# Scaled copies of the token shift in SBUF, the merged tiles split inside their own stage, and splits moved ahead of stage ends

## What is computed

```python
h = x @ w_in[l]                      # cut into rwkv, latent attention, convolution, memory and merge columns
p_prev = jnp.pad(p, ((0, 0), (1, 0), (0, 0)))[:, :-1]
p = p + mu * (p_prev - p)            # the token shift, at the start of the rwkv branch
...
branches = jnp.stack([y_rwkv, y_mla, y_conv, y_mem], axis=2)
proj = jnp.einsum('bsnc,ncd->bsnd', branches, w_o_branch[l])
gates = jax.nn.sigmoid(merge.reshape(B, S, N_BRANCH, D) + b_gate[l])
merged = jnp.sum(gates * proj, axis=2)
out = merged @ w_out[l]
x = _layer_norm(DEEPNORM_ALPHA * x + out, ln_g[l], ln_b[l])
```

## Time and profile before

| what | value |
|---|---|
| median of 3 runs (lowest to highest) | 3420.7 us (3420.3 to 3421.48) |
| the profiled execution's own time | 3420.07 us |
| its span, from the first to the last instruction | 3418.3 us |
| PE busy | 3225.6 us, 94% |
| DVE, ACT, POOL busy | 44%, 35%, 44% |
| mean granted TensorE clock | 0.982 of full speed |
| from HBM | 278.75 MB, 82 GB/s over the span |

### The profile page before, as it was taken

One profiled execution on the slowest core, in us unless ns is written; L12 is line 12 of the kernel. 1 busy time (PEld: TensorE's weight loads), 2 busy tenths in 40 slices (PEclk: granted clock), 3 DMA queues, 4 the chain that ended last, 5 costly groups with the idle time before them and its releaser, 6 DMA issues. The chain is left out here.

```text
span 3418.3 us, 51762 instructions
## 1 busy us (share of the span) xinstructions
PE 3225.6 (94%) x21116; PEld 2532.1 (74%) x21116; DVE 1500.7 (44%) x2378; ACT 1188.0 (35%) x1940; POOL 1488.2 (44%) x820
## 2 busy tenths in 40 slices
PE   8899998999898999989998988999999989899999
PEld 6784786788577747867886756888888876678787
DVE  6633374898666333848896236210000022520000
ACT  6234433422362334343223435322112233532221
POOL 4431553454344225534552258333334433845454
PEclk9999999999999999999999999999999999999999
DMA  3011121555210111325552210212111111023232
GB/s 127 9 34 55 56 99 62 209 191 200 76 62 3 39 55 51 106 86 189 200 185 85 87 32 2 68 62 62 62 62 62 62 60 56 1 87 99 93 99 93
DMA packets 77611, 284.18 MB, mean 83 GB/s; under 512 B 8736, under 2 KB 8736, under 8 KB 76864
## 3 DMA queue, kind: packets, MB, share of 16 engines
q1 hardware_dynamic: 77376, 280.88, 24.4%
HBM read 278.75 MB, written 2.10 MB: 82 GB/s over the span
## 5 line engine op out<-in xcount | busy, mean ns | idle before, releaser
L131 POOL TENSOR_TENSOR lows<-ring,highs 128x1024 fp32r<-128x1024 f32 x376 | 939.1, 2498 | 1607.3 <-ACT highs L123 1590.4
L155 PE MATMUL ps<-x_high,highs 128*128 128x512 f32 x1936 | 771.6, 399 | 36.2 <-ACT highs L123 17.4
L158 PE MATMUL ps<-x_low,highs 128*128 128x512 f32 x1936 | 758.7, 392 | 0.0
L123 ACT ACTIVATE highs<-ring 128x1024 fp32r<-128x1024 f32 x376 | 396.9, 1056 | 749.9 <-PE ps L155 388.4
L155 PEld LDWEIGHTS ps<-x_high,highs 128*128 128x128 f32 x1936 | 366.2, 189 | 127.1 <-issue 30.7
L158 PEld LDWEIGHTS ps<-x_low,highs 128*128 128x128 f32 x1936 | 365.9, 189 | 78.3 <-issue 3.5
L2744 DVE TENSOR_TENSOR hidden_scratch<-ps,hidden_scratch 128x512 f32<-128x512 f32 x44 | 30.4, 692 | 546.0 <-PE ps L2063 541.5
L677 PE MATMUL ps<-x_high,lows 128*128 128x512 f32 x1040 | 256.8, 389 | 0.0
L677 PEld LDWEIGHTS ps<-x_high,lows 128*128 128x128 f32 x1040 | 195.3, 188 | 40.5
L2620 DVE SCALAR_TENSOR_TENSOR BR<-ps,mod,BR 128x512 f32<-128x512 f32 x72 | 47.4, 662 | 368.8 <-PE ps L167 368.8
L167 PE MATMUL ps<-hidden_parts,lows 128*128 128x512 f32 (+1 forms) x528 | 188.8, 358 | 0.0
(11 more groups left out here) (435 smaller groups left out, 5917.5 us busy)
## 6 DMA issues: line engine op xcount, KB each, us to landing
ring<-in_w SPq DMA_DIRECT2D x414, 512.0 KB, 3.5
merging<-in_ada SPq DMA_DIRECT2D x48, 512.0 KB, 3.5
BR<-in_ada SPq DMA_DIRECT2D x48, 512.0 KB, 3.5
X<-in_xT SPq DMA_DIRECT2D x4, 512.0 KB, 6.7
X<-in_memT SPq DMA_DIRECT2D x2, 1024.0 KB, 5.3
merging<-in_cond SPq DMA_DIRECT2D x4, 512.0 KB, 4.7
out<-BR SPq DMA_DIRECT2D x8, 256.0 KB, 4.4
cst<-in_cst SPq DMA_DIRECT2D x1, 1408.0 KB, 7.7
```

What stands on the lines that cost most here:

```text
L123: nc.scalar.activation(self.high(n), self.chunk(n), ACT.Copy).then_inc(self.hi_made, 1)
L131: nc.gpsimd.tensor_tensor(self.low(n), self.chunk(n), self.high(n).bitcast(F32), ALU.subtract).then_inc(self.lo_made, 1)
L155: mm = nc.tensor.matmul(ps, high, xhigh, start=start, stop=False)
L158: nc.tensor.matmul(ps, high, xlow, start=False, stop=False)
```

## The change

It does six things, in both layers where nothing else is said.

- Token shift: ACT's scaled copy goes to `kept` in SBUF, two tiles in turns, in place of its bank. Its wait for its own eviction goes. PE's waits for a bank, and the one ahead of the gram matmuls, are for the copy (`kept`) and no longer for the mix.
- The first pair of tiles: PE takes k = 0, 1 of tile 0 first and waits for tile 1's high weights only after it.
- The splits of the chunk that the next stage opens with move ahead of the last evictions of ACT (latent projections, memory values).
- Merge: high and low parts of merged tiles 0 to 6 are made in the merge stage, and PE makes the high-weight matmuls of output tiles 0 and 1 for k = 0 to 6 there. To make room, `CB`, `GATE`, `WEIGHTED`, `MG` and two of the row buffers lie in the branch tiles' memory `BR`; there are three row buffers for four, three gates for four and two merged tiles for eight. SP orders its transfers anew.
- Output: x is put together (high + low) before the product arrives, so that one DVE step follows a product where there were two. The last tile isn't added to `RUN`; PE adds the sum of `RUN` and the last tile into one bank.
- Context (layer 1): its normalisation starts one output tile earlier, and its transfer waits for nothing.

```diff
-            nc.tensor.matmul(PS[:, 6, :], C("ones", P), self.run, start=True, stop=True).then_inc(S("sum"), 1)
+            nc.tensor.matmul(PS[:, 6, :], C("ones", P), self.rows[:, 7, :], start=False, stop=True, skip_group_check=True).then_inc(S("sum"), 1)
...
+        kept = X[:, 43 * T + 2 * 513:45 * T + 2 * 513].rearrange("p (c t) -> p c t", c=2)
...
+            for j, k in [(j, k) for ks in ((0, 1), *((k,) for k in range(2, DK))) for j in range(2) for k in ks]:
+                if k == 0:
+                    stream.wait_high(pe, n0 + j)
                 pe.wait_ge(before.S("x_low"), k + 1)
-                for j in range(2):
-                    with_high(nc, PS[:, j, :], tile_of(stream.high(n0 + j), k), XH[:, k, :], XL[:, k, :], k == 0)
+                with_high(nc, PS[:, j, :], tile_of(stream.high(n0 + j), k), XH[:, k, :], XL[:, k, :], k == 0)
...
-                    pe.wait_ge(R("mixed"), i - 3)
+                    pe.wait_ge(R("kept"), i - 3)
...
-                act.wait_ge(R("evicted"), i + 1)
-                a.activation(PS[:, i % 4, :], PS[:, i % 4, :], ACT.Copy, scale=less_mu[:, RW_ORDER[i]:RW_ORDER[i] + 1]).then_inc(R("kept"), 1)
+                a.activation(kept[:, i % 2, :], PS[:, i % 4, :], ACT.Copy, scale=less_mu[:, RW_ORDER[i]:RW_ORDER[i] + 1]).then_inc(R("kept"), 1)
...
-                                       in1=PS[:, i % 4, :], op0=ALU.mult, op1=ALU.add).then_inc(R("mixed"), 1)
+                                       in1=kept[:, i % 2, :], op0=ALU.mult, op1=ALU.add).then_inc(R("mixed"), 1)
...
-                pe.wait_ge(R("mixed"), RW_TILES)
+                pe.wait_ge(R("kept"), RW_TILES)
...
+                    if q == 1:
+                        stream.hi(nc, act, n0 + 11 + 1)
                     act.wait_ge(S("v"), q + 1)
                     a.activation(VV[:, q, :], PS[:, q % 2, :], ACT.Copy).then_inc(S("v_out"), 1)
-                stream.hi(nc, act, n0 + 11 + 1)
...
+                stream.hi(nc, act, nm + 8 + 1)
                 for q in range(2):
                     act.wait_ge(S("value"), q + 1)
                     a.activation(VX[:, q, :], PS[:, 4 + q, :], ACT.Copy).then_inc(S("value_out"), 1)
-                stream.hi(nc, act, nm + 8 + 1)
...
+        kept = ExitStack()
+        MH, ML = (kept.enter_context(nc.sbuf_tensor(f"merged_{part}{layer}", [P, DK, T], F32R, side="right"))[:, :, :] for part in ("high", "low"))
+
+        def flat(a, n):
+            return BR[:, a:a + n, :].rearrange("p a t -> p (a t)")
+
+        CB, GATE, WEIGHTED = flat(0, 4).rearrange("p (c k) -> p c k", c=2), BR[:, 4:7, :], BR[:, 7, :]
+        MG, PROD = BR[:, 8:10, :], flat(10, 2)
+        AD = mods[:, layer, :].rearrange("p (m c) -> p m c", c=2)
+        ROWS = (Y[:, :], flat(12, 2), flat(14, 2))
...
+                stream.send(sp, n0 + RING)
+                clear(sp, other)
+                sp.dma_start(rows_of(0), A["ada"][layer, 0, :, :]).then_inc(S("rows0"), 16)
+                sp.wait_ge(S("branch_low"), 4)
                 for c in range(2):
                     sp.dma_start(CB[:, c, :], A["cond"][c].partition_broadcast(P)).then_inc(S("cond"), 16)
...
+                for t in range(1, 48):
                     stream.send(sp, n0 + RING + 45 * t // 48)
-                    if t >= 4:
-                        sp.wait_ge(S("ada"), 2 * (t - 3))
-                    elif t >= 2:
-                        sp.wait_ge(S("branch_low"), 4 + 4 * t)
-                    sp.dma_start(rows_of(t), A["ada"][layer, t, :, :]).then_inc(S(f"rows{t % 4}"), 16)
+                    if t < 3:
+                        sp.wait_ge(S("branch_low"), 12 + 2 * t)
+                    else:
+                        sp.wait_ge(S("ada"), 2 * (t - 2))
+                    sp.dma_start(rows_of(t), A["ada"][layer, t, :, :]).then_inc(S(f"rows{t % 3}"), 16)
...
+                for t in range(2):
+                    pe.wait_ge(S("gate"), 29 + t)
+                    stream.wait_high(pe, n0 + 48 + t)
+                    for k in range(7):
+                        pe.wait_ge(S("merged_low"), k + 1)
+                        with_high(nc, PS[:, t, :], tile_of(stream.high(n0 + 48 + t), k), MH[:, k, :], ML[:, k, :], k == 0, used if t == 0 and k == 0 else None)
...
+                    if i >= 3:
+                        act.wait_ge(S("weighted"), i - 2)
+                    else:
+                        act.wait_ge(S("branch_low"), 5 + i)
+                    nc.scalar.activation(GATE[:, i % 3, :], PS[:, i % 4, :], ACT.Sigmoid, bias=par_col("b_gate", 8 * (i % 4) + i // 4)).then_inc(S("gate"), 1)
                     stream.hi(nc, act, min(gate_chunk(i) + (4 if i % 2 else 3), n0 + 48 + 1))
+                    if i >= 4 and i % 4 == 0:
+                        act.wait_ge(S("merged"), 3 * i // 4)
+                        nc.scalar.activation(MH[:, i // 4 - 1, :], MG[:, (i // 4 - 1) % 2, :], ACT.Copy).then_inc(S("merged_high"), 1)
                     if i == 0:
                         for b in range(8, 16):
                             branch_high(b)
                         act.wait_ge(S("cond"), 32)
                         nc.scalar.activation(CB, CB, ACT.Silu).then_inc(S("silu_c"), 1)
+                stream.hi(nc, act, n0 + 48 + 2)
...
+                    if i == 0:
+                        dve.wait_ge(S("branch_low"), 16)
+                    if n:
+                        dve.wait_ge(S("merged"), 3 * m + n - 1)
+                    v.tensor_tensor(WEIGHTED if n else MG[:, m % 2, :], PS[:, 4 + i % 4, :], GATE[:, i % 3, :], ALU.mult).then_inc(S("weighted"), 1)
                     if n:
                         dve.wait_ge(S("weighted"), i + 1)
-                        if n > 1:
-                            dve.wait_ge(S("merged"), 3 * m + n - 1)
-                        v.tensor_tensor(MG[:, m, :], MG[:, m, :], WEIGHTED[:, n, :], ALU.add).then_inc(S("merged"), 1)
+                        v.tensor_tensor(MG[:, m % 2, :], MG[:, m % 2, :], WEIGHTED, ALU.add).then_inc(S("merged"), 1)
...
+                    if i >= 5 and n == 1:
+                        dve.wait_ge(S("merged_high"), m)
+                        v.tensor_tensor(ML[:, m - 1, :], MG[:, (m - 1) % 2, :], MH[:, m - 1, :].bitcast(F32), ALU.subtract).then_inc(S("merged_low"), 1)
+                    for t in range(min(48, 48 * i // 29), min(48, 48 * (i + 1) // 29)):
+                        dve.wait_ge(S(f"rows{t % 3}"), 16 * (t // 3 + 1))
                         for c in range(2):
                             if 2 * t + c:
                                 dve.wait_ge(S("ada"), 2 * t + c)
                             v.tensor_tensor_reduce(PROD, rows_of(t), CB[:, c, :], 1.0, 0.0, ALU.mult, ALU.add, AD[:, t, c:c + 1]).then_inc(S("ada"), 1)
...
+                if t < 2:
+                    pe.wait_ge(S("merged_low"), 1)
+                    with_high(nc, PS[:, t, :], tile_of(stream.high(n0 + t), 7), MH[:, 7, :], ML[:, 7, :], False, stream.used if t else None)
+                    stream.wait_split(pe, n0 + t)
                     for k in range(DK):
-                        pe.wait_ge(S("merged_low"), k + 1)
-                        with_high(nc, PS[:, 0, :], tile_of(stream.high(n0), k), MH[:, k, :], ML[:, k, :], k == 0, stream.used if k == 0 else None)
-                    stream.wait_split(pe, n0)
-                    for k in range(DK):
-                        mm = nc.tensor.matmul(PS[:, 0, :], tile_of(stream.low(n0), k), MH[:, k, :], start=False, stop=(k == DK - 1))
+                        mm = nc.tensor.matmul(PS[:, t, :], tile_of(stream.low(n0 + t), k), MH[:, k, :], start=False, stop=(k == DK - 1))
...
+            pe.wait_ge(S("run"), 6)
+            nc.tensor.matmul(PS[:, 6, :], ones_matrix, RUN, start=True, stop=False, skip_group_check=True).then_inc(S("run_summed"), 1)
...
+            v.tensor_tensor(ML[:, 7, :], BR[:, 9, :], MH[:, 7, :].bitcast(F32), ALU.subtract).then_inc(S("merged_low"), 1)
             for t in range(8):
+                v.tensor_tensor(RR[:, t, :], XH[:, t, :].bitcast(F32), XL[:, t, :].bitcast(F32), ALU.add).then_inc(S("x_whole"), 1)
                 dve.wait_ge(S("product"), t + 1)
-                v.scalar_tensor_tensor(out=RR[:, t, :], in0=XH[:, t, :].bitcast(F32), scalar=DEEP_ALPHA, in1=PS[:, t % 4, :], op0=ALU.mult, op1=ALU.add).then_inc(S("residual_high"), 1)
-                dve.wait_ge(S("residual_high"), t + 1)
-                v.scalar_tensor_tensor(out=RR[:, t, :], in0=XL[:, t, :].bitcast(F32), scalar=DEEP_ALPHA, in1=RR[:, t, :], op0=ALU.mult, op1=ALU.add).then_inc(S("residual"), 1)
-                if t:
+                dve.wait_ge(S("x_whole"), t + 1)
+                v.scalar_tensor_tensor(out=RR[:, t, :], in0=RR[:, t, :], scalar=DEEP_ALPHA, in1=PS[:, t % 4, :], op0=ALU.mult, op1=ALU.add).then_inc(S("residual"), 1)
...
-            if t == 5:
+            if t == 4:
                 dve.wait_ge(S("c_in"), 16)
                 dve.wait_ge(S("c_rstd"), 1)
                 for k in range(4):
                     normed(k)
```

(2 more changed lines are left out.)

67 lines of the change are left out of this document (18 added, 49 removed).

## The result

| | before | changed |
|---|---|---|
| median (lowest to highest), 7 runs each | 3420.94 us (3420.3 to 3430.33) | 3402.9 us (3398.34 to 3411.73) |
| ratio | | 0.9946, interval 0.9935 to 0.9956 |
| profiled execution, span | 3420.07, 3418.3 us | 3402.9, 3401.1 us |

What follows compares the result with a forecast made beforehand. PE bounds the kernel, busy 3225.6 of 3418.3 us, so only its waits, matmuls and clock count. The terms sum to -33.6 us, mostly from the borders: 3420.7 - 33.6 = 3387.1 us, with 8 in 10 for 3374 to 3401.

Steps and rivals of the forecast that it cites:

- the one on the merge stage: Merge stage: DVE's seven added subtractions and ACT's seven copies a layer cost PE nothing, with three us of slack.
- The start of the merge stage: Gate product 2's chunk, sent behind row 1, lands later: a loss of 1.3 us a layer (0 to 2.5), +2.6 in all.
- Opening: Layer 0's start: four matmuls run ahead and the clock may rise sooner, -1.4 us (0.9 to 2.1 gained).
- Token shift: Token shift: ACT's copy into SBUF gives -0.2 us, mixes of tiles 9 and 10 under POOL +1.2, both layers together.
- Rival 4: Token shift: mixes wait out POOL in every tile and DVE passes it on; 3423 us or more, chance 0.03.
- The moved splits: Latent stage and memory values: earlier splits shorten PE's border waits, -6.9 and -5.8 us over two layers.
- the clock, 0.7 a pair of borders: Latent and memory borders: shorter PE waits may keep the clock up, 0 to 2 us a pair, -1.4 in all.
- Merge to output: Border from merge to output stage: 28 matmuls follow at once, one wait remains; -6.5 us a layer, -13.0 in all.
- End of the output stages: Output stages' ends: fewer DVE steps on the path, shorter waits, some clock; -2.5 us in layer 0, -6.2 in layer 1.
- (2): Merge stage gets tight: ACT's wait for the merged tile or DVE's eighth step delays high splits; 3401 us, chance 0.13.
- (1): At the borders the clock stays up and POOL isn't in the way; 3369 us, around 3374 for most, chance 0.13.
- (3): Latent and memory borders: moved splits do nothing, since another engine ends the stage as late; 3401 us, chance 0.04.

Runs made afterwards that it cites:

- merged_copy_later: The changed kernel with ACT's high copy of a merged tile moved behind the next gate and its split: 3405.82 us, ratio 0.9957.
- moved_splits_alone: The kernel before with only the two moved splits (latent stage, memory values): 3409.38 us, ratio 0.9968.
- also_at_the_start: The changed kernel with every merge-stage weight chunk sent one row earlier, gate product 2's ahead of row 1's wait too: 3388.91 us, ratio 0.9911.

## Why the prediction was wrong, step by step

**The step that failed** is the one on the merge stage, "so I cost it at nothing". It priced the work that was added to ACT and DVE, and found it harmless, rightly: the copy moved away gave next to nothing back, and with SP's chunk a row earlier PE had no wait in the steady part although all the added work was there. What it did not price is the place of the weight chunks in SP's queue. It did look at SP's order, but only at the start, with "Behind SP's wait stand also row 2 and the next chunk, which have 5 us to spare". With three row buffers for four every row, and every chunk behind it, waits until one row more is summed, and this was not followed past the start. Measured were +12.5 and +10.4 us for the stages in place of +1.3 each: 7.0 and 6.2 in the steady part, which was forecast at nothing, and 5.5 and 4.2 at the start. The chunk a row earlier gave the steady part back whole. The start came back with the two further edits, by stage length 9.2 us with its chunk (3.6 of them because PE reached gate product 2 earlier, the rest with the clock) and 3.2 with the split ahead of the silu. With these the time is 3380.8; the forecast for a merge stage at nothing was 3387.1 - 2.6 = 3384.5.

**The start of the merge stage** was forecast as a loss of 1.3, a term that was mis-sized. In layer 0, PE reached gate product 2 2.7 us later by its marks (21.50 us from the start for 18.81). It ran the first part behind it, to the next L1658, in 17.55 in place of 14.74 us, at the lower level: 0.79 and then 0.63 us a record where there were 0.50 and then 0.39. That makes 5.5 in all, where my upper end was 2.5. The stage also opens partly at the lower level (0.64 at 586.55 for 0.47 at 597.31), 1.6 us longer to the first pair of branch products. But this cost nothing, since PE waits for the chunk behind it anyway: in the run merged_copy_later the stage opened at the full level, PE's wait was 4.72 us in place of 3.12, and it reached gate product 2 after 21.47 us.

**Opening**: -1.4 forecast, -1.8 measured. PE starts at 7.72.

**Token shift**: the size was right, +1.0 forecast, no difference measured, and the reason half right. The mixes with two inputs in SBUF do wait out POOL. DVE's groups, changed kernel:

```profile
L845 DVE SCALAR_TENSOR_TENSOR X<-X,par 128x512 f32<-128x512 f32 x26 | 25.0, 963 | 42.8 <-ACT X L797 42.8
```

and before:

```profile
L846 DVE SCALAR_TENSOR_TENSOR X<-X,par,ps 128x512 f32<-128x512 f32 x26 | 19.3, 743 | 50.5 <-ACT ps L798 50.5
```

Five of the 26 did so. In layer 0 tile 1 took 1.44 us, tile 5 2.89 and tile 9 1.78 (at 88.89, beside the first of POOL's four operations of 1.74 us from 88.37 on); in layer 1 tile 1 took 1.43 and tile 9 1.78. Of tiles 9 and 10, where I had put them at +0.73 each, tile 9 came 1.05 us longer and tile 10 met nothing (0.74 at 98.42, POOL's split having ended at 97.95). The times show no cost of them, and DVE has 43 us of idle time ahead of the mixes. By the rule of the Trainium skill (SBUF — State Buffer, "Who interferes with whom"), that a VectorE instruction with two SBUF inputs and a GpSimd one that reads SBUF get in each other's way, such mixes had to come; the trace agrees. Rival 4 failed because five of 26 met POOL and not all, and those had DVE's idle time ahead of them. That the size came out is in part luck. PE's gram wait fell from 4.33 to 2.76, but a new one of 1.61 for L883 stands 4 us ahead of it. ACT's scaled copy was not cheaper in SBUF:

```profile
L797 ACT ACTIVATE X<-ps,less_mu 128x512 f32<-128x512 f32 x26 | 17.7, 681 | 0.0
```

It takes 0.68 for 0.66 in its bank. The prediction's "about 0.60" took a copy without a scale for one with it. The page on ScalarE that I had set aside, by which ScalarE is faster into PSUM than into SBUF, was right in its sign (the Trainium skill, ScalarE: Activation LUTs, "Step-by-step: what each stage is for"). The 0.1 us a tile came from the wait that went: the second copy starts 0.50 behind the first, not 0.63.

**The moved splits**: the waits as forecast (0.94 and 1.23 for "about 1 and 1.5"), 3.5 and 3.1 us. The term mis-sized is the clock, 0.7 a pair of borders: behind the latent border the attention ran 3.0 us faster, since the lower level that it had before is not there (L330's row is 1.55 us for 2.90). These 3.0 us (12.2 for 15.2 from the border to 335.33) are the same in layer 0 of all eleven kernels with the moved splits. The lower level at the start of the merge stage is not their price: the run moved_splits_alone opens it at the full level in both layers, as do the runs also_at_the_start and merged_copy_later. Alone the edit gave 12, forecast 14.1.

**Merge to output**: -6.5 a layer, forecast -6.5, and by the forecast's own steps: one wait of 3.23 us (3.3), with DVE's last low part at 2.23 us beside POOL's 2.34.

**End of the output stages**: -8.6 in the trace and -10.6 alone, forecast -8.7. That the sum fits is in part luck. In layer 0 PE's wait fell by 2.2 us (2.50 to 0.32) where I had 1.4, and the clock helped more. In layer 1 the 1.39 is gone, but the last wait is 2.15 us where I had left 1.1, and the clock helped less, so the piece gave 4.7 and not 6.2.

**The rivals**: (2) had the right place and, by chance, nearly the right time, 3401, but not the cause; its cause was seen only where DVE was made slower. (1) and (3) are out, (4) as told.

## What to carry to other kernels

When a change takes a buffer away from one stream, follow the queue that serves it: what stands behind its wait in the same queue, above all the weights of the bounding engine, is late by one turn as well. The remedy cost nothing here: it is to issue the critical transfer ahead of the wait. And compare stages by their length between marks, not by the waits alone: here the borders gained 43 us in all, and one stage between them took 23 of it, while PE's waits for high weights had grown by only 7 us in the list. Last, look at a piece that no edit touches before reading a small difference of whole times: here the second block alone varied by 10 us.

## What the runs showed of the hardware

- The ada sum (two inputs of 128x1024 in SBUF) takes 1.22 us where POOL is idle, and 3.18 us from 698.82 on in the changed kernel, beside POOL's split from 697.92 to 700.91; the longest took 3.43. Writing its product in bf16 leaves it at 1.23.
- The mix takes 0.74 us with both inputs in SBUF and POOL idle, and up to 2.89 beside POOL's work. With one input in PSUM all 26 took 0.73 to 0.75, beside POOL's work or not.
- The same kernel's time moves with the clock that it is granted. The changed kernel took 3398.34 us at a mean of 0.988 and 3411.73 at 0.981; of the kernel before, six of seven runs lie between 3420.3 and 3421.48 and one is 3430.33. Where a wait of 4.42 us became one of 0.94, behind the latent stage, the clock stayed up (3.0 us gained). The length of a wait alone doesn't say which level follows: behind 3.12 us at gate product 2 the next records ran at the lower level in the changed kernel, behind 3.21 us in also_at_the_start at the full one.
